# Two Transformer blocks on one core: a mixture-of-experts loop entered in another order, its shared second product moved behind round 1, its three-expert rounds moved to the odd places

## What is computed

```python
scores = sigmoid(xf @ w_router)                      # 256 x 64
biased = scores + b_router
# per token: the 4 best of 8 groups (sum of a group's 2 best), then the 8 best experts in them
w = chosen scores / their sum * 2.5
routed = sum over the chosen experts e of w[e] * ((silu(x @ w1[e]) * (x @ w3[e])) @ w2[e])
shared = (silu(xf @ ws1) * (xf @ ws3)) @ ws2
y = routed + shared
```

## Time and profile before

| | |
|---|---|
| median of 3 runs | 2012.62 us (2004.08 to 2015.46) |
| the profiled execution's own time | 2008.7 us |
| its span | 2006.8 us |
| TensorE busy | 1819.2 us (91%) |
| VectorE, ScalarE, GpSimd busy | 915.9, 360.7, 55.0 us |
| granted clock, mean | 0.95 |
| moved by DMA | 586.38 MB, mean 292 GB/s |
| first layer: entry and loop | about 339 to 856 us of the span |
| second layer: entry and loop | about 1162 to 1676 us |

### The profile page before, as it was taken

One profiled execution on the slowest core, in us unless ns is written; L12 is line 12 of the kernel. 1 busy time (PEld: TensorE's weight loads), 2 busy tenths in 40 slices (PEclk: granted clock), 3 DMA queues, 4 the chain that ended last, 5 costly groups with the idle time before them and its releaser, 6 DMA issues. The chain is left out here.

```text
span 2006.8 us, 27853 instructions
## 1 busy us (share of the span) xinstructions
PE 1819.2 (91%) x10492; PEld 1043.2 (52%) x10492; DVE 915.9 (46%) x2058; ACT 360.7 (18%) x701; POOL 55.0 (3%) x166
## 2 busy tenths in 40 slices
PE   5999999989879878889999989888788787999998
PEld 3847884443433334376588644333333333585485
DVE  2897532543433433369874253433433423451351
ACT  2143112011111111123231011111111112141131
POOL 1000002000000000000000010000000001010000
PEclk9999999999989989999999999989989988998998
DMA  9655637899999999957455449999999998333430
GB/s 348 205 215 184 235 126 282 340 421 420 421 421 420 420 420 421 409 179 218 168 215 203 190 169 419 421 421 420 420 421 420 421 420 239 109 116 109 155 105 21
DMA packets 146471, 586.38 MB, mean 292 GB/s; under 512 B 12844, under 2 KB 17568, under 8 KB 96416
## 3 DMA queue, kind: packets, MB, share of 16 engines
q1 hardware_dynamic: 144928, 581.47, 74.5%
q0 software_dynamic: 1408, 3.10, 0.6%
HBM read 583.49 MB, written 1.05 MB: 291 GB/s over the span
## 5 line engine op out<-in xcount | busy, mean ns | idle before, releaser
L1385 PE MATMUL banks<-weight_ring,x_units 128*32 128x512 f32 x2560 | 418.3, 637 | 0.2 <-DMA weight_ring<-in_w 0.2
L1385 PE MATMUL banks<-spare_slot,x_units 128*32 128x512 f32 x768 | 221.0, 740 | 96.3 <-DMA weight_ring<-in_w 96.3
L2163 DVE TENSOR_TENSOR sig_h<-banks,sig_h 128x256 f32<-128x256 f32 x52 | 22.1, 425 | 413.6 <-ACT sig_h L1672 413.6
L1385 PEld LDWEIGHTS banks<-spare_slot,x_units 128*32 128x32 f32 x768 | 58.2, 132 | 255.3 <-issue 255.3
L1385 PEld LDWEIGHTS banks<-weight_ring,x_units 128*32 128x32 f32 x2560 | 109.9, 117 | 131.9 <-issue 131.2
L1043 PE MATMUL banks<-h_t,weight_ring 128*128 128x256 f32 x768 | 170.1, 380 | 0.0
L1043 PEld LDWEIGHTS banks<-h_t,weight_ring 128*128 128x128 f32 x768 | 145.3, 190 | 21.3 <-issue 1.6
L2442 PE MATMUL banks<-weight_ring,h_t 128*128 128x512 f32 (+2 forms) x384 | 134.1, 509 | 0.5 <-DMA weight_ring<-in_w_in 0.5
L983 PE MATMUL banks<-h_t,weight_ring 128*128 128x256 f32 x512 | 113.9, 385 | 3.7 <-DVEq L1740 3.7
L1409 PE MATMUL banks<-qk,conv 128*32 128x512 f32 x448 | 94.3, 594 | 22.0 <-issue 22.0
L1422 PE MATMUL banks<-o_parts,slot_of 128*128 128x512 f32 x416 | 110.6, 406 | 3.1 <-DVE o_parts L2200 3.1
(11 more groups left out here) (509 smaller groups left out, 2413.5 us busy)
## 6 DMA issues: line engine op xcount, KB each, us to landing
weight_ring<-in_w SPq DMA_DIRECT2D x208, 1024.0 KB, 17.4
weight_ring<-in_w_in SPq DMA_DIRECT2D x36, 2048.0 KB, 12.8
slots<-in_w SPq DMA_DIRECT2D x52, 1024.0 KB, 20.7
weight_ring<-in_w_mod SPq DMA_DIRECT2D x24, 2048.0 KB, 12.4
spare_slot<-in_w SPq DMA_DIRECT2D x48, 1024.0 KB, 11.2
qk<-in_w SPq DMA_DIRECT2D x26, 1024.0 KB, 21.4
h_t<-in_w SPq DMA_DIRECT2D x26, 1024.0 KB, 14.0
qk_t<-in_w SPq DMA_DIRECT2D x24, 1024.0 KB, 14.7
```

The source lines that it names most:

```text
L1385: mm = nc.tensor.matmul(h_bank[own, :], x_blk[:, i, k, own], w13(p % RING_X)[:, :, k, :], start=(k == 0), stop=(k == KT - 1), skip_group_c ...
L2163: v.tensor_tensor(act_pair, h_bank[:, 0:FF], sig_pair, ALU.mult)
```

## The change

It reorders the entry and the loop; the two layers' results stay the same sums. Loads: w2 of experts 0 and 1 are issued behind the mixer's last weights; the next layer's parameters behind chunk ("gt", 1, 0), earlier in the layer; only three experts are loaded ahead of the table; w13 and w2 of expert 3 come behind w13 of place 4; w2 of place 4 comes behind w13 of place 8. TensorE: mod("rt") goes behind the router and behind the wait for the shared weights; shared_h is cut at other places; the overflow product comes last of the list; the turn of the shared activations goes from the gathers to behind round 0's first product, and shared_second behind round 1's. ScalarE copies chunk 14's columns out of PSUM, and VectorE reduces them ahead of shared_act(1) instead of inside the choice. VectorE's choice loses five small instructions (three of the groups' comparison, two of the masking). PLAN: rounds 2 and 4 have two experts with one of them in three tiles, the other even rounds two, and the odd rounds from 3 three.

The diff, cut to its core (the constants that follow PLAN and the new signals' definitions are left out):

```diff
     rounds, at = [], 0
     for n in range(26):
-        if n < 2 or (n % 2 and n > 5):
+        if n in (2, 4):
+            kind = (0, 0, 0, 1)
+        elif n % 2 == 0 or n < 2:
             kind = (0, 0, 1, 1)
-        elif n % 2 == 0:
+        else:
             kind = (0, 0, 1, 2)
-        else:
-            kind = (0, 0, 0, 1)
         rounds.append([at + j for j in kind])
...
-        + [("xT", 1, g) for g in range(4)] + mod_groups("turned", layer) + ["rt_halves"] + mod_groups("rt", layer) + ["rt"]
+        + [("xT", 1, g) for g in range(4)] + mod_groups("turned", layer) + ["rt_halves", "rt"] + mod_groups("rt", layer)
...
-        sh_turned_at = [o_bank2[:, 0:2 * P], h_bank[:, 0:2 * P]]
+        sh_turned_at = [o_bank2[:, 0:2 * P], x_bank[:, 0:2 * P]]
...
+        if name == ("gt", 1, 0) and l + 1 < DEPTH:
+            sp.wait_ge(B[l]["vec"].full, B[l]["vec"].full_at(l))
+            load_conv_params(ds(l + 1, 1))
+            sp.wait_ge(col_ready[1].sem, col_ready[1].at(l))
+            load_mod_params(ds(l + 1, 1))
         if name == ("wo", 1):
+            sp.wait_ge(B[l]["y", 2, 1, 1].full, B[l]["y", 2, 1, 1].full_at(l))
+            sp.wait_ge(oa_ready.sem, oa_ready.at(l))
+            expert2(l, 0, 0)
+            expert2(l, 1, 1)
...
-    for e in range(FORMED):
+    for e in range(FORMED - 1):
         before = loads[l][len(loads[l]) - RING + e][3]
-        if before is None:
-            sp.wait_ge(sh_h_done.sem, sh_h_done.at(l, T))
-        elif before[0] == "mod_dve":
+        if before[0] == "mod_dve":
             sp.wait_ge(dve_parts.sem, dve_parts.at(l, before[1] - DVE_CHUNKS[0] + 1))
         else:
...
             sp.wait_ge(B[l][before].full, B[l][before].full_at(l))
         expert13(l, e, e)
-    sp.wait_ge(B[l]["y", 2, 1, 1].full, B[l]["y", 2, 1, 1].full_at(l))
-    expert2(l, 0, 0)
-    expert2(l, 1, 1)
     sp.wait_ge(B[l]["wo", 1, 1].full, B[l]["wo", 1, 1].full_at(l))
     expert2(l, 2, 2)
-    sp.wait_ge(sh_h_done.sem, sh_h_done.at(l, T))
-    expert2(l, 3, 3)
-    if l + 1 < DEPTH:
-        load_mod_params(ds(l + 1, 1))
-        load_conv_params(ds(l + 1, 1))
     sp.wait_ge(table_ready.sem, table_ready.at(l))
...
-    def load_rest(at):
-        held = None
+    def load_rest(at, first=False):
+        held = {}
         for p in range(FORMED, N_EXPERTS):
-            e = expert_of(p)
+            e = held[p] = expert_of(p)
             if p >= RING_X:
                 sp.wait_ge(h_done, at(NR, LAST_ROUND[p - RING_X] + 1))
                 sp.sem_inc(wait_carrier, 1)
             expert13(l, e, p % RING_X)
-            if held is not None:
-                load_second(at, held, p - 1)
-            held = e
-        load_second(at, held, N_EXPERTS - 1)
+            if p == FORMED and first:
+                sp.wait_ge(sh_h_done.sem, sh_h_done.at(l, T))
+                expert13(l, 3, 3)
+                expert2(l, 3, 3)
+            for q in {6: [5], 7: [6], 8: [4, 7]}.get(p, [p - 1] if p > 8 else []):
+                load_second(at, held.pop(q), q)
+        load_second(at, held.pop(N_EXPERTS - 1), N_EXPERTS - 1)
...
     mm.then_inc(B[l]["rt_halves"].full, 1)
-    mod("rt")
     pe.wait_ge(rt_moved.sem, rt_moved.at(l))
...
-    for b in list(B[l]["=moe_y", t, h] for t in range(T) for h in range(2)):
+    def moe_y_free(t, h):
+        b = B[l]["=moe_y", t, h]
         pe.wait_ge(b.free, b.free_at(l))
     pe.wait_ge(C[l]["shared"].filled, C[l]["shared"].filled_at(l))
-    shared_h(0, range(KT))
+    moe_y_free(1, 0)
+    if l + 1 < DEPTH:
+        mod("rt")
+    shared_h(0, range(0, 5))
...
     mm.then_inc(count_done.sem, 1)
-    moe_free(3)
-    shared_h(1, range(0, 1))
+    shared_h(0, range(5, 7))
     moe_free(0)
     pe.wait_ge(place_ready.sem, place_ready.at(l))
...
         mm = nc.tensor.transpose(h_bank[:, t * P:(t + 1) * P], place_64[:, t].rearrange("p i e -> p (i e)"),
                                  K.ident[:])
     mm.then_inc(place_turned.sem, 1)
-    shared_h(1, range(1, 2))
+    shared_h(0, range(7, 8))
+    moe_y_free(0, 0)
     pe.wait_ge(to_col_ready.sem, to_col_ready.at(l))
     pe.wait_ge(place_t_ready.sem, place_t_ready.at(l))
...
         mm = nc.tensor.matmul(cols_bank[:, at_cols + t * COLS:at_cols + (t + 1) * COLS], place_t[e64, t, :], to_col[e64, :],
                               start=True, stop=True)
     mm.then_inc(cols_done.sem, 1)
-    pe.wait_ge(over_ready.sem, over_ready.at(l))
-    nc.tensor.matmul(o_bank[:, at_over:at_over + PASSES - 1], K.ones[e64, :], over[e64, :], start=True, stop=True)
     for t in range(T):
         nc.tensor.matmul(h_bank[:, at_cols + t * COLS:at_cols + (t + 1) * COLS], place_t[second64, t, :], to_col[second64, :],
                          start=True, stop=True)
-    nc.tensor.matmul(o_bank[:, 0:COLS], K.part[e64, 0:1].to_broadcast([N_EXPERTS, P]), to_col[e64, :], start=True,
-                     stop=True).then_inc(list_done.sem, 1)
+    nc.tensor.matmul(o_bank[:, 0:COLS], K.part[e64, 0:1].to_broadcast([N_EXPERTS, P]), to_col[e64, :], start=True, stop=True)
+    moe_free(3)
+    shared_h(1, range(0, 2))
+    pe.wait_ge(over_ready.sem, over_ready.at(l))
+    nc.tensor.matmul(o_bank[:, at_over:at_over + PASSES - 1], K.ones[e64, :], over[e64, :], start=True, stop=True)\
+        .then_inc(list_done.sem, 1)
     shared_h(1, range(2, KT))
+    moe_y_free(0, 1)
+    moe_y_free(1, 1)
...
         gather(0, 0)
         gather(0, 1)
-        pe.wait_ge(act_cleared, at(1, 1))
-        for t in range(T):
-            shared_turn(t)
         for q in (2, 3):
             pe.wait_ge(x_ready, quarter(0, q - 2))
             gather(0, q)
-        pe.wait_ge(sh_act_t_ready, at(T, T))
+        pe.wait_ge(sh_act_ready.sem, sh_act_ready.at(l, T))
         turn_slots(0)
...
             first_product(n)
             if n == 0:
+                pe.wait_ge(act_cleared, at(1, 1))
+                pe.wait_ge(weight_ready, at(TURNS, 1))
+                for t in range(T):
+                    shared_turn(t)
+                pe.wait_ge(sh_act_t_ready, at(T, T))
+            if n == 1:
                 pe.wait_ge(shared2_gated.sem, shared2_gated.at(l))
                 for t in range(T):
                     shared_second(t)
...
-            if n == 0:
-                pe.wait_ge(weight_ready, at(TURNS, 1))
-            elif following and i > 0:
+            if following and i > 0:
                 pe.wait_ge(weight_ready, at(TURNS, it + 2))
             second_product(n)
...
     act.drain().then_inc(rt_moved.sem, 1)
-    if following:
-        copy_mod(15)
     bank = full_of("rt", l)
     nc.scalar.activation(score[:], bank[:, 0:T * N_EXPERTS].rearrange("p (t n) -> p t n", t=T), ACT.Sigmoid)\
         .then_inc(B[l]["rt"].free, 1)
     act.drain().then_inc(score_ready.sem, 1)
+    if following:
+        copy_mod(15)
+        bank = full_of(("mod_cols", 14), l)
+        copy_out(("mod_cols", 14), l, cols_kept, bank[:])
+        act.drain().then_inc(cols_moved.sem, 1)
...
-        for t in range(T):
-            act.wait_ge(sh_turned, at(T, t + 1))
-            nc.scalar.activation(act_t[:, t], sh_turned_at[t].rearrange("p (f n) -> p f n", f=2), ACT.Copy)\
-                .then_inc(sh_act_t_ready, 1)
         for n in range(NR):
...
             sigmoid(n)
+            if n == 0:
+                for t in range(T):
+                    act.wait_ge(sh_turned, at(T, t + 1))
+                    nc.scalar.activation(act_t[:, t], sh_turned_at[t].rearrange("p (f n) -> p f n", f=2), ACT.Copy)\
+                        .then_inc(sh_act_t_ready, 1)
...
-    if l + 1 < DEPTH:
-        mod(14)
     v.tensor_tensor(g_score[:], top[:, :, :, 0], top[:, :, :, 1], ALU.add)
     dve.drain()
-    for t in range(T):
-        other, own = broadcast(g_score[:, t, :], 1, N_GROUPS), broadcast(g_score[:, t, :], 2, N_GROUPS)
-        v.tensor_tensor(g_cmp[:, t], other, own, ALU.is_gt)
-        v.tensor_tensor(g_eq[:, t], other, own, ALU.is_equal)
-    dve.drain()
-    for t in range(T):
-        v.tensor_tensor(g_eq[:, t], g_eq[:, t], K.lower8[:], ALU.mult)
+    other, own = broadcast(g_score[:], 2, N_GROUPS), broadcast(g_score[:], 3, N_GROUPS)
+    v.tensor_tensor(g_cmp[:], other, own, ALU.is_gt)
+    v.tensor_tensor(g_eq[:], other, own, ALU.is_equal)
+    dve.drain()
+    v.tensor_tensor(g_eq[:], g_eq[:], broadcast(K.lower8[:], 1, T), ALU.mult)
     dve.drain()
...
-    v.tensor_scalar(g_rank[:], g_rank[:], TOPK_GROUPS - 0.5, None, ALU.is_lt)
-    dve.drain()
-    v.tensor_scalar(g_neg[:], g_rank[:], -NEG, NEG, ALU.mult, ALU.add)
+    v.tensor_scalar(g_neg[:], g_rank[:], TOPK_GROUPS - 0.5, 2.0 * NEG, ALU.subtract, ALU.mult)
+    dve.drain()
     by_group = biased[:].rearrange("p t (g e) -> p t g e", g=N_GROUPS)
-    v.tensor_tensor(by_group, by_group, broadcast(g_rank[:], 3, PER_GROUP), ALU.mult)
-    dve.drain()
-    v.tensor_tensor(by_group, by_group, broadcast(g_neg[:], 3, PER_GROUP), ALU.add)
```

(24 more changed lines are left out.)

20 lines of the change are left out of this document (11 added, 9 removed).

## The result

The changed kernel takes 2018.17 us (median of 9 runs, 2017.19 to 2030.23), the kernel before 2005.56 us over 9 runs as well (2001.21 to 2015.46). The ratio is 1.0065, 95% interval 1.0039 to 1.0091: slower by 0.65%. Forecast was 2021 (2004 to 2033), with 0.42 for slower by over 0.5% and 0.50 for within it. The interval takes in 0.5%, so it is not settled on which side of that bound the change lies. The profiled execution of the changed kernel is one of these runs (2017.19 us, span 2015.4).

What follows compares the result with a forecast made beforehand. TensorE's path to round 2's first product, which releases place 9's load, was taken to bound the loops once DMA is full. Entries +2.5 and +5.8 and rounds +3.2 gave +11.5 us on 2008.7, forecast 2021 us (2004 to 2033).

Steps and rivals of the forecast that it cites:

- The bound: Both loops: the later of DMA backlog and round 2's first product, which frees place 9's slot, sets the loop's end.
- the margin of the first layer: First layer: place 9's load could flow at 422.3, loads ahead of it end at 425.3, so 3.0 us of delay is free.
- First layer, the path: First-layer entry on TensorE: round 2's first product 5.5 us later; less the 3.0 us margin, +2.5 us.
- counts: First layer: counts start at 360.0 against 360.52; second layer: the choice before them is 0.7 us shorter.
- counts to round 0's first product: First layer: list read 2.4 us later plus chunk 14's 1.9; second layer: 2.7 + 1.1 + 0.5, plus 1.0 for half clock.
- the shared turn: Turn of shared activations behind round 0's first product: no longer hidden by the wait for blocks, costs 1.2 us per layer.
- Second layer, the path: Second-layer entry on TensorE: round 2's first product 5.8 us later, with no DMA margin, so +5.8 us.
- The rounds: Loop's end: TensorE stands before round 25, which then runs at half clock for 9.6 us; +1.6 us per layer, 3.2 together.
- the signs named ahead: Counts at 360, round 0's first product 380 to 381, place 9's load near 426 and 1248, DMA holes, stops before odd rounds.
- Early loads that pay: Rival: round 2's first product is not the gate, place 9's load flows 7.9 and 4.5 us sooner; 1999.5 us, 12%.
- Half the entry's cost: Rival: entry terms are smaller, about +2 us per layer's entry and nothing behind; 2013 us, 28%.
- Half clock spreads: Rival: new TensorE stops (before shared weights, behind turned places, before blocks) bring half clock, 2.5 us more per entry; 2025 us, 15%.

Runs made afterwards that it cites:

- The load run: Kernel before with only the change's early loads (parameters, first w2 loads, table's first load sooner), engine orders and rounds kept: 2006.16 us, ratio 0.9989.
- shared product late: Kernel before with the shared second product behind round 2's first product and w2 of place 4 loaded behind w13 of place 9: 2009.88 us, ratio 1.0008.
- both: Kernel before with the change's early loads and the shared second product moved behind round 2's first product: 1996.99 us, ratio 0.9948.
- other order of loads: Kernel before with early loads and late shared second product, but w2 of place 4 queued behind w13 of place 10: 2008.92 us, ratio 1.0014.
- the shorter choice: Kernel before with early loads, late shared product and the change's shortened VectorE choice: w2 of place 4 behind w13 of place 10 2006.93 us, ahead of it 1995.01.

## Why the prediction was right

**The bound.** Right. In the kernels with the old rounds in which w2 of place 4 lands in time, the loop is nearly a constant behind place 9's issue wherever that is late: 422.4 to 423.3 in six of seven such loops, 424.2 in one. Put at 415 us for the 166 loads behind place 9, DMA's full rate ended some 414.3 to 415.5 us behind its issue in the second layers of six kernels (from 1 us windows). Against the changed kernel with the old rounds, the margin of the first layer, put at 3.0, is 425.5 - 422.4 = 3.1 (2.2 by the longest of the six), and that of the second, put at nothing, is 0.1. What the prediction did not see is that the same first product frees the slots of places 9, 10 and, with the old rounds, 11: the place of w2 of place 4 in the queue, which it never had to price, decides over those.

**First layer, the path.** Put at +5.5, measured +7.5. By its terms:
- counts: put at 0.5 sooner, measured 2.0 later. **This step failed.** It let mod("rt") run behind TensorE's stop for the weights at the speed of the earlier trace rows: part 15 takes 3.64, not 1.92, and its sums begin at half clock (0.50 from 351 to 357), right behind 3.90 us of standing; with the piece ahead of the stop again, part 15 took 1.92. Part 15 and the sums take 358.62 - 353.09 = 5.5 in place of 3.6, which is 1.9 of the 2.5; the rest is the weights' landing, 6.97 behind the router's product in place of 6.32.
- counts to round 0's first product: put at +4.8 (the list's 4.3 and 0.5), measured 20.09 - 15.88 = +4.2. The hop behind the sigmoid, put at 1.1, is 0.84 (the row of L1315).
- the shared turn: put at 1.2, measured 45.10 - 43.86 = +1.2 from the start of round 0's first product to place 9's issue.

**Second layer, the path.** Put at +5.8, measured +5.8: counts -0.65 (put at -0.7), counts to first product 22.75 - 17.44 = +5.3 (put at 2.7 + 1.1 + 0.5 + 1.0), shared turn +1.1 (put at 1.2). The standing of 4.20 (put at 3.9) was followed by half clock through 1188 to 1194, as said. Undoing the split alone took 4.2 of it away.

**The rounds.** Put at +1.6 in each layer; putting the old rounds back took 3.0 and 0.9 from the loop behind place 9's load, 3.9 together against 3.2. Round 25's first product took 9.77 and 9.17, put at 9.6; the mechanism is as said, DMA stops of 7.50 and 6.08 ahead of it.

**The sum.** Put at +11.5 on the loops, measured +7.4 and +6.6 = +14.0 behind the router's product. By its terms: 7.5 - 3.1 + 3.0 = 7.4 in the first layer and 5.8 - 0.1 + 0.9 = 6.6 in the second. The failed step is 2.5 too little and the rounds 0.7; the list gives 0.6 back and the margins 0.2, which leaves 0.1 unplaced. The profiled executions then differ by only 8.6 in their spans, in the main because of the half-clock stretch of the kernel before; the medians differ by 12.6. The prediction's own base was the profiled 2008.7, above the median of 9 runs, so 2021 lies 3 above what was measured. That the forecast step of 12.3 us (2008.7 to 2021) is so near to 12.6 is in part luck: the loops cost 2.5 us more than was put. Of the signs named ahead, the holes, the stops ahead of odd rounds and round 25's length came as said; counts, round 0's first product and place 9's load in the first layer came 3.0, 2 to 3 and 2.2 us later than said. Place 9's load of the second layer, put near 1248, went at 1256.43, of which 8.2 us are the later start of that whole entry.

**The rivals.** Early loads that pay: fallen, the load run alone gives 0.9989. The load run also bears out what was set against the Trainium skill's advice to issue early ("DMA: Bandwidth & Descriptors", "Rules for kernel authors"): the table's first load went out 15.7 us earlier, and nothing came of it that the interval shows, while a slot's release stood between. Half the entry's cost: fallen, the path cost 13.3 us where 11.3 were forecast. Half clock spreads: right for one of its three stops. It came behind the stop for the shared weights, for which it was not priced in the forecast, and neither behind the turned places (0.84 us) nor behind the stop ahead of the blocks (1.30 in the first layer). The Trainium skill's rule ("TensorE: Matmul & The Clock Gate", "Why this matters for your kernels") warns of long idle gaps between bursts of matmuls, not of short ones. The 3.90 and 4.20 us here agree with it; the half clock behind the shorter stops of the last section is not covered by it.

## What to carry to other kernels

When a slot's release gates the loads, find the one release at which the queue's backlog and the compute path meet; moving only one of them bought nothing here, and moving both 0.5%, with the old rounds and entry; with the new ones it bought nothing, for the next slot's release stood behind. Work that covers a wait for data must stay ahead of that wait: behind it, it cost its time again here, and at half clock (5.5 us in place of 3.6). Before a load with its own condition is moved within an in-order queue, list what stands behind it and who needs what it brings: one position was worth 12 us in each of two pairs of kernels (1996.99 and 2008.92, 1995.01 and 2006.93).

## What the runs showed of the hardware

- **The same short stops are sometimes followed by half clock and sometimes not.** Five kernels have the entry of the kernel before, with the long choice, and in the first layer two stops of TensorE, ahead of the first shared product and behind it, that add up to 1.6 us in each. With 0.19 and 1.43 us (the kernel before) and with 0.84 and 0.77 (early loads) the clock stayed up, and counts to round 0's first product took 15.9 us. With 0.72 and 0.90 (shared product late), 0.35 and 1.27 (both) and 0.71 and 0.90 (other order of loads, with one more stop of 1.43 us before them) the window from 363 to 366 was granted 0.50, and it took 17.1: the stretch costs 1.2 us each time. With the shorter choice the second stop was 0.25 us in one run and none in the other, and the clock stayed up in both (15.9 and 15.8). So neither the sum nor the longer of the two stops tells which are followed by half clock; what does stays open. TensorE's rows with the shared product late and, behind them, with the early loads, and the window at half clock of the former:

```profile
352.71 7.11 PE L1269 MATMUL banks<-weight_ring,h_t 128*128 128x512 f32 x16 [0.72 <-DMA weight_ring<-in_ws]
360.72 0.41 PE L1281 MATMUL banks<-spare_slot,strict 128*128 128x64 f32 x2 [0.90 <-DVEq L2055]
```

```profile
355.23 7.11 PE L1272 MATMUL banks<-weight_ring,h_t 128*128 128x512 f32 x16 [0.84 <-DMA weight_ring<-in_ws]
363.10 0.41 PE L1284 MATMUL banks<-spare_slot,strict 128*128 128x64 f32 x2 [0.77 <-DVEq L2058]
```

```profile
363.00:366.00 3.00, 3.00 (x6) 1.26 (x6) 2.15 (x8) 0.38 (x1) 0.00 (x0) 0.50 0.74 306
```

- **The same kernel's executions scatter by more than this change.** 13 to 14 us from the lowest to the highest of 9 runs in either kernel; two sources that can make such scatter are in the traces, the entry's start (344.57 to 348.04 in five kernels with the same code up to there) and the second block's stretch at half clock with TensorE busy for 9.11 of 10 us (3.9 us in the trace of the kernel before). What starts that stretch stays open.
